# Expert 0's bias behind its first product, the token count behind the second chunk, the first gather over two waits

## What is computed

```python
h2 = rmsnorm(x, ffn_norm_g)
logits = h2 @ router_w + router_b                 # 256 x 32
topv, topi = top_k(logits, 4)
topw = softmax(topv)
combine = sum(one_hot(topi, 32) * topw[..., None], axis=1)
for e in range(32):
    gu = h2 @ w1[e] + b1[e]                       # 1024 x 2048
    gate = minimum(gu[:, :1024], 7.0)
    lin = clip(gu[:, 1024:], -7.0, 7.0)
    act = (lin + 1) * gate * sigmoid(1.702 * gate)
    out += combine[:, e:e+1] * (act @ w2[e] + b2[e])   # 1024 x 1024
x = x + out
```

## Time and profile before

| | us |
|---|---|
| median of 3 runs | 1095.99 |
| lowest, highest | 1095.63, 1096.5 |
| the profiled execution | 1095.41 |
| its span, first to last instruction | 1093.70 |
| TensorE busy (matmuls) | 1059.5 |
| VectorE, ScalarE, GpSimd busy | 269.3, 174.8, 47.0 |

### The profile page before, as it was taken

How to read it: one execution, slowest core, us unless ns; L and a number is a source line. 1 busy time by engine, 2 the same in 40 slices (tenths; PEclk the granted TensorE clock), 3 DMA queues, 4 the chain that set the end, 5 groups by cost and what they waited for, 6 DMA issues and landing times.

```text
span 1093.7 us, 11756 instructions
## 1 busy us (share of the span) xinstructions
PE 1059.5 (97%) x4874; PEld 411.1 (38%) x4874; DVE 269.3 (25%) x562; ACT 174.8 (16%) x385; POOL 47.0 (4%) x38
## 2 busy tenths in 40 slices
PE   9999999999999999999999999999899998999998
PEld 7455446433333333333333333333333333333332
DVE  4986552311111111111111111111111111111111
ACT  3253313111111111111111111111101111111112
POOL 0637000000000000000000000000000000000000
PEclk9999999999999999999999999999999999999999
DMA  9933587999999999999999999999999999999997
GB/s 337 366 128 126 228 336 288 388 424 429 428 416 423 432 430 432 428 432 431 434 430 427 435 434 430 433 431 431 430 433 431 434 428 433 431 434 429 427 427 297
DMA packets 34314, 432.57 MB, mean 396 GB/s; under 512 B 3548, under 2 KB 5104, under 8 KB 17648
## 3 DMA queue, kind: packets, MB, share of 16 engines
q1 hardware_dynamic: 32096, 430.73, 93.4%
q10 hardware_dynamic: 2192, 1.48, 0.5%
HBM read 431.15 MB, written 1.05 MB: 395 GB/s over the span
## 4 chain that ended last, share of the span: by engine, by line
PE 66%; DMA 33%; DVE 0%; issue 0%; SPq 0%; POOL 0%; POOLq 0%; DVEq 0%
DMA ring<-in_expert_w_dram 33%; PE bank L468 24%; PE bank L497 14%; PE bank L1539 11%; PE bank L506 4%; PE bank L431 3%; PE bank L1760 3%; PE bank L458 2%; PE bank L445 1%; PE bank L480 1%; PE bank L450 1%; PE bank L1505 0%; PE bank L438 0%; PE bank L1487 0%; PE bank L1510 0%; PE bank L1497 0%
## 5 line engine op out<-in xcount | busy, mean ns | idle before, releaser
L468 PE MATMUL bank<-ring,work 128*64 128x512 f32 x2048 | 449.8, 594 | 15.6 <-DMA ring<-in_expert_w_dram 15.5
L468 PEld LDWEIGHTS bank<-ring,work 128*64 128x64 f32 x2048 | 142.9, 137 | 318.9 <-issue 288.3
L497 PE MATMUL bank<-ring,work 128*64 128x512 f32 x992 | 219.5, 593 | 12.4 <-DMA ring<-in_expert_w_dram 12.4
L1379 DVE TENSOR_SCALAR work<-bank 128x512 f32<-128x512 f32 x31 | 21.4, 692 | 457.3 <-PE bank L468 457.3
L497 PEld LDWEIGHTS bank<-ring,work 128*64 128x64 f32 x992 | 75.2, 137 | 152.2 <-issue 149.9
L1539 PE MATMUL bank<-ring 128*128 128x512 f32 x224 | 99.1, 596 | 0.0
L972 ACT ACTIVATE work<-work 128x512 f32<-128x512 f32 x31 | 19.5, 630 | 480.1 <-DVE work L1379 480.1
L532 DVE TENSOR_TENSOR work<-bank,vecs 128x512 f32<-128x512 f32 x31 | 21.4, 692 | 213.5 <-PE bank L445 213.5
L506 PE MATMUL bank<-work,putT 64*128 64x512 f32 x248 | 61.9, 616 | 0.0
L1539 PEld LDWEIGHTS bank<-ring 128*128 128x128 f32 x224 | 41.7, 190 | 49.0 <-issue 48.6
L431 PE MATMUL bank<-xs,pick 128*64 128x512 f32 x248 | 58.5, 592 | 0.0
(11 more groups left out here) (247 smaller groups left out, 521.2 us busy)
## 6 DMA issues: line engine op xcount, KB each, us to landing
ring<-in_expert_w_dram SPq DMA_DIRECT2D x70, 4096.0 KB, 39.5
ring<-in_expert_w_dram SPq DMA_DIRECT2D x43, 2048.0 KB, 14.0
ring<-in_w_in_dram SPq DMA_DIRECT2D x8, 2048.0 KB, 21.0
ring<-in_expert_w_dram SPq DMA_DIRECT2D x13, 1024.0 KB, 10.3
ring<-in_w_out_dram SPq DMA_DIRECT2D x2, 2048.0 KB, 10.7
ring<-in_w_branch_attn_dram SPq DMA_DIRECT2D x1, 2048.0 KB, 7.9
ring<-in_w_branch_pool_dram SPq DMA_DIRECT2D x1, 2048.0 KB, 12.7
work<-in_expert_w_dram SPq DMA_DIRECT2D x2, 1024.0 KB, 13.2
```

What stands on the lines that cost most here:

```text
L468: mm = pe.matmul(dst, hTe[:, at:at + SLOTS], w[a][:, col:col + BANK], start=(k == 0 and not bias_first), stop=(k == KD - 1 and bias_first) ...
L497: mm = pe.matmul(ps[SLOTS * half:SLOTS * (half + 1), :], actT[:, at:at + SLOTS], w[a // 2][:, col:col + BANK], start=(k == 0), stop=(k == ...
```

## The change

Four steps move; none is added or taken away.

- `up_bias` of expert 0 stood ahead of the gather. It now stands behind the four chunks of `up`, closes the sums and raises `gemm1`. The first product of each sum opens it in its place (`bias_first=False`).
- `count_tokens` stood behind the gather, and now stands behind chunk 1 of expert 0's `up`.
- Ahead of `place_tokens(1)` stood two of the gather's eight products of tile 0; now there are six. The last two stand behind it, ahead of the wait for `first_pick` 2.
- VectorE wrote the one-hot of expert 1 (`build_bias_pick(1)`) ahead of expert 0's SwiGLU. It now does so behind it, since expert 0's bias reads the same tile until then.

```diff
@@ -1418,7 +1418,6 @@
             build_put(slot_id, 0).then_inc(put_ok, 1)
-            build_bias_pick(1).then_inc(s["bias_ok"], 1)
 
@@ -1431,6 +1430,7 @@
             def expert(e, wide, gain_at, first=False):
                 glu(e, wide)
                 if first:
+                    build_bias_pick(1).then_inc(s["bias_ok"], 1)
                     rows_in(1, gain_at)
@@ -1858,22 +1858,19 @@
             route(range(6, 8))
-            pe.wait_ge(s["bias_ok"], 1)
-            up_bias(pe)
             pe.wait_ge(s["first_pick"], 1)
-            gather_first(pe, 0, 0, range(0, 2))
+            gather_first(pe, 0, 0)
+            gather_first(pe, 0, 1, range(0, 2))
             place_tokens(1)
-            gather_first(pe, 0, 0, range(2, 4))
-            gather_first(pe, 0, 1)
+            gather_first(pe, 0, 1, range(2, 4))
             pe.wait_ge(s["first_pick"], 2)
             gather_first(pe, 1, 0).then_inc(first_gathered, 1)
             gather_first(pe, 1, 1).then_inc(rowsT_ps, 1)
-            count_tokens()
-
-            def up_early(w, c):
-
-                up(pe, w, c, range(0, 1)).then_inc(half_used, 1)
-                return up(pe, w, c, range(1, W1_ROWS))
+
+            def up_early(w, c, bias_first=True):
+
+                up(pe, w, c, range(0, 1), bias_first).then_inc(half_used, 1)
+                return up(pe, w, c, range(1, W1_ROWS), bias_first)
 
@@ -1893,10 +1890,13 @@
                     if c == 2:
                         pe.wait_ge(hTe_ok, 1)
-                    mm = up_early(w, c)
+                    mm = up_early(w, c, bias_first=False)
                     if c < W1_CHUNKS - 1:
                         mm.then_inc(chunk_used, 1)
-                mm.then_inc(gemm1, 1)
+                    if c == 1:
+                        count_tokens()
+                pe.wait_ge(s["bias_ok"], 1)
+                up_bias(pe, first=False).then_inc(gemm1, 1)
```

## The result

Over 20 runs the changed kernel takes 1100.06 us in the median (1097.12 to 1103.92), the kernel before 1096.67 (1095.08 to 1098.14, 20 runs): a ratio of 1.0032 with a 95% interval of 1.0023 to 1.0040, 3.5 us slower. The forecast was 1096.4 us, the range ended at 1098.0. The changed kernel also spreads over 6.8 us where the one before spreads over 3.1.

The account below looks back on a forecast made before the run. The prediction took the 431 GB/s stream of expert weights as the bound. An early-start gain cut to 0.1 us against 0.5 us for a partial restart gave +0.4 us, so 1096.4 us; the range ended at 1098.0 us.

Follow-up runs that it names:

- narrow filler: Kernel before with expert 0's bias and the one-hot copy moved, plus four 128x64 gather products repeated ahead of the gather: 1098.83 us, ratio 1.0029.
- three gathers and the queue opened: Kernel before with expert 1's gather done three times, and chunk 32 and each loop turn's first-step w1 and w2 transfers issued piecewise: 1099.55 us, ratio 1.0026.
- the opened change: Changed kernel with chunk 32 and each loop turn's first-step w1 and w2 transfers issued piecewise as slots free: 1100.34 us, ratio 1.0033 to the kernel before.

## What to carry to other kernels

Before moving a wide product out of a stretch of narrow ones, look at what is left. The 512-wide work that seems to be a mere microsecond of cost can be what keeps TensorE's clock at 1.00 (here 2 of 165 runs fell with it, 26 of 53 without), and busy time in the profile does not show it. When a stream is fed by an engine, reckon issued less moved bytes at every issue up to where the engine waits for the stream, not only near the edit; the thinnest place sets how much lag is free. A copy that must wait for a tile's last reader moves a wait: here a second tile removed it.

## What was unexpected of the hardware

- The granted clock went to 0.50 while TensorE was busy without a gap: near 191.1 us behind router and gather products of 32 and 64 columns, and back to 1.00 near 198 us in the 512-wide weight products. With the bias alone moved (and a wait of 0.79 us ahead) it stayed at 0.50 from 191 to beyond 200 us.
- It differs from run to run of one kernel: 11 of 20, 6 of 6, 4 of 11, 2 of 12 and 0 of 11 runs for kernels that differ by a microsecond of work or its order. A single profile of such a kernel can show either side, as the narrow filler's did.
- A queue that runs down and goes on from half chunks of 1024 KB lost 1.5 to 2.2 us of a 431 GB/s stream. With three gathers and the queue opened it was nearly empty for one of these (66 and 33 GB/s from 218.5 to 219.5 us); in the opened change no half microsecond was below 164 GB/s, and 2.0 us were lost all the same.
